# The output projection of two pooled groups by seven block products a half, with split tokens summed on VectorE, GpSimd and ScalarE

## The reference

```python
def pool_mixer(h, w_in, w_group, scale, w_out):
    B, S, _ = h.shape
    u, z = jnp.split(h @ w_in, 2, axis=-1)
    p = causal_multiscale_pool(u).reshape(B, S, N_POOL_GROUPS, GROUP_WIDTH)
    y = jnp.einsum('bsgc,gcd->bsgd', p, w_group).reshape(B, S, A_WIDTH_2) * scale
    return (y * jax.nn.silu(z)) @ w_out
```

## Time and profile before

| | us |
|---|---|
| median of three runs | 2352.72 |
| the profiled execution | 2353.32 |
| its span in the trace | 2351.4 |
| TensorE busy | 2324.9 |
| VectorE busy | 1537.1 |
| GpSimd busy | 1255.9 |
| ScalarE busy | 859.8 |

### The profile page before, as it was taken

The page is one execution under the profiler, slowest core; times in us unless marked ns, Lnnn a source line. Parts: engine busy times, 40 slices in busy tenths (PEclk is TensorE's granted clock), DMA queues, the critical chain, the costliest instruction groups (busy, mean ns, idle before and its releaser), DMA issues.

```text
span 2351.4 us, 32286 instructions
## 1 busy us (share of the span) xinstructions
PE 2324.9 (99%) x11585; PEld 1943.6 (83%) x11585; DVE 1537.1 (65%) x1839; ACT 859.8 (37%) x1596; POOL 1255.9 (53%) x724
## 2 busy tenths in 40 slices
PE   9999999999999999999999999999999999999998
PEld 7888789888888888888888888788878788889887
DVE  7825555524578777877877777774672967147885
ACT  5212555512543222222222443122231244157773
POOL 4533954143135666676777424573754733467743
PEclk9999999999999999999999999999999999999999
DMA  6511001031011333333332211112121123210034
GB/s 220 157 45 50 19 19 37 1 117 54 10 42 50 117 125 125 117 124 125 117 123 63 63 45 45 59 57 73 54 81 62 58 67 110 79 37 25 22 112 139
DMA packets 67420, 179.08 MB, mean 76 GB/s; under 512 B 7010, under 2 KB 13924, under 8 KB 65200
## 3 DMA queue, kind: packets, MB, share of 16 engines
q1 hardware_dynamic: 57840, 148.03, 19.3%
q10 hardware_dynamic: 9104, 27.51, 3.5%
q0 software_dynamic: 368, 2.10, 0.5%
HBM read 161.84 MB, written 15.77 MB: 76 GB/s over the span
## 4 chain that ended last, share of the span: by engine, by line
PE 76%; DVE 6%; issue 4%; POOL 2%; ACT 1%; DMA 0%; POOLq 0%; DVEq 0%; ACTq 0%; SPq 0%
PE ps L705 21%; PE ps L706 21%; PE ps L708 21%; PE ps L855 4%; PE ps L833 3%; PE ps L843 2%; DVE trail L3538 1%; PE ps L2410 1%; POOL split_lo L1658 1%; PE ps L2426 1%; ACT p L956 1%; PE ps L2395 1%; PE ps L2396 1%; PE ps L2425 1%; PE ps L509 0%
## 5 line engine op out<-in xcount | busy, mean ns | idle before, releaser
L705 PE MATMUL ps<-h_hi,split_hi 128*128 128x512 f32 x1546 | 607.2, 393 | 3.4 <-DVE h_lo L3220 1.3
L706 PE MATMUL ps<-h_lo,split_hi 128*128 128x512 f32 x1546 | 601.9, 389 | 0.0
L708 PE MATMUL ps<-h_hi,split_lo 128*128 128x512 f32 x1546 | 536.5, 389 | 0.0
L1516 POOL TENSOR_TENSOR split_hi<-raw,cf 128x1024 fp32r<-128x1024 f32 x64 | 125.2, 1956 | 427.8 <-PE ps L708 373.2
L705 PEld LDWEIGHTS ps<-h_hi,split_hi 128*128 128x128 f32 x1546 | 290.9, 188 | 63.9 <-issue 2.2
L708 PEld LDWEIGHTS ps<-h_hi,split_lo 128*128 128x128 f32 x1546 | 290.9, 188 | 61.0
L706 PEld LDWEIGHTS ps<-h_lo,split_hi 128*128 128x128 f32 x1546 | 291.2, 188 | 56.3 <-issue 0.2
L1605 POOL TENSOR_TENSOR split_lo<-raw,split_hi 128x512 fp32r<-128x512 f32 x144 | 232.9, 1635 | 193.9 <-ACT split_hi L2723 193.4
L1658 POOL TENSOR_TENSOR split_lo<-raw,split_hi 128x512 fp32r<-128x512 f32 x84 | 128.1, 1534 | 179.2 <-ACT split_hi L2884 179.2
L2723 ACT CAST split_hi<-raw 128x512 fp32r<-128x512 f32 x144 | 86.7, 622 | 283.9 <-PE ps L708 204.0
L1518 POOL TENSOR_TENSOR split_lo<-raw,split_hi 128x1024 fp32r<-128x1024 f32 x64 | 178.4, 2787 | 5.0
(11 more groups left out here) (508 smaller groups left out, 5213.2 us busy)
## 6 DMA issues: line engine op xcount, KB each, us to landing
raw<-in_strips SPq DMA_DIRECT2D x208, 256.0 KB, 2.8
raw<-in_strips SPq DMA_DIRECT2D x86, 512.0 KB, 3.4
ada_raw<-in_ada SPq DMA_DIRECT2D x64, 512.0 KB, 3.7
memw_raw<-in_mem_strips SPq DMA_DIRECT2D x8, 512.0 KB, 6.1
xT<-in_xT ACTq DMA_DIRECT2D x4, 1024.0 KB, 8.1
x_spill_d<-xT ACTq DMA_DIRECT2D x1, 3584.0 KB, 10.1
xT<-x_spill_d ACTq DMA_DIRECT2D x2, 1792.0 KB, 9.9
out_T<-out_sb SPq DMA_DIRECT2D x13, 256.0 KB, 2.2
```

Of the source, the lines that this page charges most:

```text
L705: pe.matmul(acc[:, a:b], w_hi, hi[:, a:b], start=first, stop=False)
L706: pe.matmul(acc[:, a:b], w_hi, lo[:, a:b], start=False, stop=False)
L708: mm = pe.matmul(acc[:, a:b], w_lo, hi[:, a:b], start=False, stop=last)
L1516: pool.tensor_tensor(hi, raw[:, r, :], ones[:, 0:1].to_broadcast([P, D]), ALU.mult).then_inc(hi_split, 1)
```

## The change

The output projection of groups two and three (g = 1 and 2) is done by seven block products as well. The eight output tiles fall into two "quads" of four; in each, the weights of 512 inputs by 512 outputs are four blocks of 256 by 256, and the tokens are two halves of 512 by two halves of the inputs. A product (quad, i) has two parts (output tiles) of two input tiles, 12 matmuls, so 2 x 7 x 12 = 168 matmuls in place of 192. Group four and group one keep the eight tiles.

- TensorE goes through the products in the order of `OUT_ORDER`: (0,0), (0,1), then (1,0), moved over from the second quad, (0,2) to (0,6), and (1,1) to (1,6). Products 2, 4 and 6 add onto the PSUM of 0, 2 and 4, once VectorE has read that.
- The tokens: products 0 and 3 take the gated tiles of the first 512 tokens; 1 and 5 tiles of the second 512, where tiles 0 and 1 have had the first 512 tokens' values subtracted (`first_difference`); 2, 4 and 6 take sums called neg 2, neg 3 and neg 4, two tiles each. VectorE makes neg 2 (`neg_two`) and the first tile of neg 4; GpSimd makes neg 3 and the second tile of neg 4. ScalarE casts their high parts and VectorE makes the low parts (`neg_low`).
- The sums live where the second 512 tokens of tiles 0 to 5 of `h_hi` and `h_lo` are (`h_plain` is the same memory in fp32). These are stored to DRAM once (`h_keep_d`, in group two), fetched back after each of the two projections and rounded again by ScalarE before the next group's sixth and seventh product (`h_rounded`).
- VectorE reads each product out of PSUM as two half-width parts (`out_sum`), 28 a group in place of 8 full ones.
- The loops over the groups on TensorE and GpSimd are written out. GpSimd makes the weight sums of the two quads (`out_forms`), SyncE loads strips 12 and 13 as the first quad's places come free.

```diff
+OUT_BANKS = (((4, 6), (5, 7), (2, 3)), ((0, 1), (5, 7), (2, 3)))
+OUT_ORDER = [(0, 0), (0, 1), (1, 0)] + [(0, i) for i in range(2, 7)] + [(1, i) for i in range(1, 7)]
+OUT_AFTER = {2: 0, 4: 2, 5: 1, 6: 4}
...
+            def load_out(g, quad):
+                for i, d in ((2, 0), (3, 1), (4, 2), (6, 3)):
+                    group_split(sp, g, out_form(quad, i))
+                    load_group_half(g, 12 + 2 * quad + d // 2, d % 2)
...
+            def out_forms(g, quad):
...
+                pool.tensor_tensor(pool_form, a21, a22, ALU.add).then_inc(form_sum, 1)
+                out_low(1)
+                if quad == 0:
+                    early_half(pool, g)
+                    out_low(0, 1)
+                summed(g, 4 + quad, 1)
+                pool.tensor_tensor(a21, a21, a11, ALU.subtract).then_inc(form_sum, 1)
+                group_split(pool, g, out_form(quad, 1))
+                pool.tensor_tensor(pool_form, a11, pool_form, ALU.subtract).then_inc(form_sum, 1)
+                for kk in range(2 if quad == 0 else 0):
+                    if kk == 0:
+                        gate_high(pool, g, 3)
+                    neg_made(pool, g, 1 + 2 * kk)
+                    pool.tensor_tensor(neg_full(g, 3, kk), neg_full(g, 2, kk), neg_full(g, 3, kk), ALU.add).then_inc(neg_rest, 1)
+                    if kk:
+                        gate_made(pool, g, 5)
+                        pool.tensor_tensor(neg_full(g, 4, kk), neg_full(g, 2, kk), gates[:, 2 + kk, 0:HALF], ALU.add).then_inc(neg_rest, 1)
+                    if kk == 0:
+                        out_low(2)
...
+            def out_forms_of(g):
...
+                    if quad == 0:
+                        if i in (2, 4, 6):
+                            neg_lower(pe, g, i)
+                        else:
+                            gate_lower(pe, g, {0: 1, 1: 4, 3: 6, 5: 7}[i])
...
+                        slot, w = group_at(g, p)
+                        product(pe, bank(OUT_BANKS[quad][OUT_BANK[i]][part]), slot,
+                                [(w + 2 * part + kk, *out_token(g, i, kk)) for kk in range(2)], HALF, start=i in (0, 1, 3), skip=True)\
+                            .then_inc(form_done if part else pool_tile, 1)
...
                     if p == GROUP_OUT_AT + 3:
                         group_through(act, g, GROUP_TILE_AT + 3)
...
+                        if g < POOL_GROUPS - 1:
+                            neg_high_tile(g, 2, 1)
                     group_high(g + p // GROUP_FORMS, p % GROUP_FORMS)
...
+            def out_tokens_made(g):
+
+                first_difference(g, 0)
+                first_difference(g, 1)
+                gates_low(g, 3, y_lo[:, 0:2, t1], gates[:, 0:2, t1], y_hi[:, 0:2, t1])
+                gate_step(g, 2).then_inc(pool_g, 1)
...
+                neg_two(g, 0)
+                neg_made(dve, g, 1)
+                difference_low(g, 0)
+                dve.tensor_tensor(neg_full(g, 4, 0), neg_full(g, 2, 0), gated_tile(2)[:, t1], ALU.add).then_inc(neg_sum, 1)
+                gates_low(g, 4, y_lo[:, 2, t2], gated_tile(2)[:, t2], gated_hi_tile(2)[:, t2])
+                gate_step(g, 3, t2).then_inc(pool_g, 1)
+                gate_made(dve, g, 4)
+                neg_two(g, 1)
+                neg_made(dve, g, 3)
+                difference_low(g, 1)
+                gate_step(g, 3, t1).then_inc(pool_g, 1)
+                neg_low(g, 2, 0)
+                neg_low(g, 2, 1)
+                out_sum(g, 0, 0, 0)
+                out_sum(g, 0, 0, 1)
+                gates_low(g, 4, y_lo[:, 2, t1], gated_tile(2)[:, t1], gated_hi_tile(2)[:, t1])
+                gates_low(g, 6, y_lo[:, 3, t1], gated_tile(3)[:, t1], gated_hi_tile(3)[:, t1])
+                neg_low(g, 3, 0)
+                neg_low(g, 3, 1)
+                out_sum(g, 0, 2, 0)
...
```

More of the change, by code:

```diff
@@ L692, in build, with product @@
                           lambda k: adav[:, 24 + k:25 + k], n_kv, tmp5)
-        def product(pe, acc, slot, pieces, width=T, before=None, free=None, start=True, stop=True, weights=(split_hi, split_lo)):
+        def product(pe, acc, slot, pieces, width=T, before=None, free=None, start=True, stop=True, weights=(split_hi, split_lo), skip=False):
             spans = [(a, min(a + HALF, width)) for a in range(0, width, HALF)]
@@ L1450, in _ @@
                 load_group(g)
[L1451 to L1454, removed]
+                group_split(sp, g, out_form(1, 0))
+                load_group_half(g, 10, 1)
+                for quad in range(2):
+                    load_out(g, quad)
+            load_group(POOL_GROUPS - 1, True)
+            for d in range(4):
+                group_split(sp, POOL_GROUPS - 1, GROUP_OUT_AT + d)
+                load_group_half(POOL_GROUPS - 1, 12 + d // 2, d % 2)
             for r in range(2):
@@ L1664, in _ @@
+            for g in range(1, POOL_GROUPS):
                 for q in range(4):
@@ L1681, in _ @@
                         group_low(g, at + f, POOL_SOURCE[f])
-                for d in range(12):
+                for d in range(4 if g < POOL_GROUPS - 1 else 12):
                     group_half(pool, g, 8 + d // 2, d % 2)
                     group_low(g, GROUP_TILE_AT + d, raw_half(d // 2 % 2, d % 2))
+                for quad in range(2 if g < POOL_GROUPS - 1 else 0):
+                    out_forms(g, quad)
             for r in range(2):
@@ L2905, in _ @@
                     group_high(g, p)
-                act.wait_ge(pool_res, 8 * g)
+                out_read(act, g, 0)
                 act.dma_start(x_pair_d, xT[:, 6:8, :]).then_inc(x_spilled, 16)
-                for p in range(4, GROUP_FORMS + (4 if g < POOL_GROUPS - 1 else 0)):
+                forms = GROUP_FORMS + 4 if g < POOL_GROUPS - 1 else GROUP_OUT_AT + 8
+                for p in range(4, forms):
                     if p < GROUP_TILE_AT and p % 7 == 4:
@@ new lines, in _ @@
+                    if g == 1 and p in (8, 10, 12, 14, 16, 18):
+                        m, low = 2 + (p - 8) // 4, (p - 8) // 2 % 2
+                        sums_made(act, 1, 12)
+                        act.dma_start(h_keep_d[:, low, NEG_T[m]:NEG_T[m] + 2, :],
+                                      rows((h_hi, h_lo)[low][:, NEG_T[m]:NEG_T[m] + 2, HALF:T])).then_inc(h_kept, 16)
+                    if g > 1 and p == 5:
+                        act.wait_ge(h_again, 64 + 64 * (g - 1))
+                        h_round(2)
@@ L3711, in _ @@
                 last_products(g, 3, gated_tile(2), gated_tile(3))
+                if g < POOL_GROUPS - 1:
+                    out_tokens_made(g)
+                    for quad in range(2):
+                        for i in range(7) if quad else (5, 6):
+                            for part in range(2):
+                                out_sum(g, quad, i, part)
+                    continue
                 for t in range(4):
```

302 lines of the change are left out of this document (254 added, 48 removed).

## The result

The changed kernel takes 2357.64 us (median of 20 runs, 2355.60 to 2359.82), the kernel before 2352.45 in the same comparison (20 runs): a ratio of 1.0020, 95% interval 1.0014 to 1.0026. It is slower by 5.2 us between the medians, and by 4.7 us (3.3 to 6.1) by the ratio. The forecast was 2362, that is 9.4 slower: the sign was right and so was the mechanism in the main, but the size was about twice what came. The profiled execution took 2357.31 us. The clock of TensorE has a part in the spread: the changed kernel's 8 executions with a mean granted clock of 0.999 average 2356.6 us, the other 12, at 0.996 to 0.998, 2358.2.

What follows compares the result with a forecast made beforehand. TensorE, busy 2324.9 of 2351.4 us, was taken as the bound. Waits of 10.1 us a group against 5.4 saved gave +4.7, twice +9.4, on 2353.3: 2362.7, forecast as 2362 us, range 2345 to 2367.

Steps and rivals of the forecast that it cites:

- What it takes away: Output projections of groups two and three: 24 matmuls fewer a group, 5.44 us each, -10.88 us for two groups.
- Step 1: Product (0,1): VectorE's four operations take turns with GpSimd's, so tile 1's difference comes late; TensorE waits 2.4 us.
- Step 2: Product (0,2): neg 2's second low part waits behind token sums and a weight sum, then a residual; 2.2 us.
- Step 3: Rest of the first quad: waits of 1.7 at (0,3), 0.5 at (0,4), 0.1 at (0,5), 3.1 us at (0,6).
- sum of 10.1: All waits of a group's projection added, with rounding, 10.1 us against 5.4 saved: +4.7 a group.
- upper bound: Most wait per group: a full turn lost at each handover, 0.1 more at each TensorE start; about 12 us.
- The edits at no cost: Token stores, fetches with ScalarE's rounding, and strip loads hidden; written-out loops change nothing, within 1 us.
- The token sum on VectorE: VectorE makes one of four token sums beside GpSimd's three; gains 0.6 us of shared turns a group.
- A: Rival: tokens come in time in the projections, 1 us of wait per group, faster at 2344 us; chance 0.16.
- B: Rival: no change, waits about equal the gain, tokens late only at (0,2), weights then limit; 2354.5 us; chance 0.18.
- C: Rival: TensorE's clock falls too behind long waits, about 1.5 us a group behind (0,6); 2365 to 2368 us; chance 0.08.

Runs made afterwards that it cites:

- e1: Changed kernel with GpSimd making the first quad's second and third weight sums ahead of the low part of (1,0); 2352.08 us, ratio 0.9997 to the kernel before.
- e2: Changed kernel with GpSimd waiting in the first quad for both low parts of neg 2 before its fourth weight sum; 2354.97 us, ratio 1.0014.
- e8: Changed kernel with three clears of an unused buffer (some 0.2 us) on VectorE in group three, before its second running mean's first pass; 2358.53 us, ratio 1.0021.
- e5: e4 with ScalarE's rounding of h for tile 4 split, its low half one form later; 2345.61 us, ratio 0.9972.
- e7: e4 without the fetch of h back and its roundings, so values of groups three and four differ; 2345.49 us, ratio 0.9973.
- e4: Changed kernel with e1's move, ScalarE's cast of form (0,2) before neg 2's second tile, and VectorE's first residuals between neg 2's low parts; 2347.41 us, ratio 0.9978.
- e6: Changed kernel with both token sums of neg 4 on GpSimd, VectorE's one moved back; 2356.82 us, ratio 1.0020.
- e3: Changed kernel with the eight weight sums of each of the two projections made on 16 of 512 columns; 2348.45 us, ratio 0.9982.

## Why the prediction was right in sign and wrong in size

**What it takes away.** 5.44 us a group: right. TensorE's projection has 168 matmuls in place of 192, and without waits they keep the old pace: the 84 from 1638.42 to 1657.58 take 19.16 us, 0.228 each.

**Step 1, (0,1): 2.4 forecast, 1.99 measured.** Right in every link: the releaser is VectorE's low part of tile 1's difference, behind four operations in turns with GpSimd's four. These took 5.97 (1608.01 to 1613.98) where 6.37 was reckoned, which is all of the 0.4; e1 removes the cause and the wait goes.

**Step 2, (0,2): 2.2 forecast, 1.66 measured.** The weight sum (1620.90) does stand ahead of neg 2's second low part (1621.04, 1.70), and the residual behind it releases TensorE; e2 takes that sum away and the delay falls by 0.95.

**Step 3 failed in size.** (0,3) was forecast at 1.7 and measured at 1.08; (0,4) 0.5 and 0.16; (0,5) 0.1 and 0.63; and the one that fell furthest, (0,6), 3.1 and 1.66. The forecast had VectorE reach neg 4's low parts 24.6 us after zero and lose two full turns, until 28.4. In the trace it reached them at 23.5 (1635.08 - 1611.62), while GpSimd had just waited 0.78 for a cast and was near the end of a low part (1634.07, 1.30). So the first of the two met the rest of a turn and only the second a whole one: 2.53 for both, where 3.8 were reckoned.

So the sum of 10.1 failed by two terms. (0,6), charged with two whole turns, is 1.4 of the 2.9 us by which the six delays (7.2) fall short of it. The other is the price of a pair of turns, 1.70 for 1.90: it makes the 0.4 at (0,1), and its share in the 0.5 at (0,2) and the 0.6 at (0,3) is argued from the same count and not shown by itself. With the 0.1 at each start, which the forecast had only in its upper bound, the lateness is 7.9. Rows 5 and 6 already showed a pair at less than its parts: GpSimd's 1549.61 lasts 2.27 beside VectorE's 1548.42 and 1550.77 of full width, and 1.22 and 1.25 make 2.47. Over the two groups the waits beyond the gain come to 2.4 and 1.8, 4.3 in place of 9.4.

**The edits at no cost** were nearly that. The stores, the fetch (12 of 512 KB, 4.7 us) and the written-out loops show no wait, and TensorE doesn't wait at the sixth and seventh products of groups three and four. The rounding on ScalarE was not hidden in group four: its quads lose 0.6 in the changed kernel's profile (79.30 against 78.73) and 0.4 in e8's (79.09), and e5 and e7 remove 0.74 and 0.77 of e4's. Group three's quads lose 0.4 (e8) for a reason that stays open. These terms of about 1.0 were missing, and with them the sum from rows is 4.3 + 1.0 = 5.3, near the 5.2 measured.

**The token sum on VectorE** was priced at 0.6 us a group; e6 shows no difference.

**The rivals.** A fell: the lateness is 7.9 and 7.3 a group and not 1, and without the weight sums (e3) it is still 3.5. B's size was closer to the result than the forecast's (its sum is 2354.6 and not 2354.5), but not its mechanism: in the changed kernel the second quad's weights never limit, and only in e4's profile does (1,2) wait for one, 1.08. Of C, the clock did fall behind two of the long waits in this profile, once hidden as the prediction said of waits ahead of other late products and once, behind the wait in group three's quads, at a cost of 1.7; behind (0,6) it did not fall. Its premise that the waits of steps 1 to 3 are longer than 1.92 us held for (0,1) alone. C has a part in the time even so: executions of the kernel before at a mean clock of 0.999 average 2352.5 (24 of the 33 measured with e1 to e4), those of the changed one 2356.6 (8 of 20). At that clock the two are 4.1 apart, so up to 1 us of the 5.2, by this estimate, goes with lower clocks.

## What to carry to other kernels

When two engines alternate, count turns, but price them from a contended pair from start to start (here 1.70), not as the sum of the two free times; and charge a whole turn only where the other engine has its next operation queued without a wait. Here a saving of matmuls was lost by the order of small work around it and won back there: with the work unchanged, three moves of order and one split took the change from 5.2 us slower to 6.6 us faster (e5, 2345.61 against 2352.20). Look first at what GpSimd has queued in front of the first product that needs VectorE.

## What the runs showed of the hardware

- An operation of GpSimd on 16 columns takes 0.21 us by itself and 0.67 to 0.76 beside VectorE's operations on SBUF (e3); on 512 columns it is 1.28 and 1.74 (changed kernel). The surplus of about 0.5 us for the turn doesn't shrink with the columns.
- Of a contended pair VectorE's half-width operation adds 0.45 us to GpSimd's 1.25, where it takes 0.69 by itself: 1.70 from start to start.
- Which engine goes first at a meeting can differ between two executions of the same instructions: in group three GpSimd's weight sum was 0.03 us ahead of VectorE's pass in the changed kernel's profile and 0.29 behind it in e8's, before e8's edit acts, and took 1.29 and 2.16.
- The clock fell in the changed kernel behind waits of 2.02 (third quad of group three) and 1.98 us ((0,1), group three), but not behind one of 1.99 ((0,1), group two) of the same profile. It fell behind one of 2.00 in e6 and not behind the 1.99 at (0,1) in either group of e2 and e8. The fall at 1358 in the profile of before shows in e1, e2, e4 and e5 and is absent in the other six.
